# A retention layer's per-head steps, some of them moved to a later slot between the matmuls

## The chip, the cores and the metric

One Trainium2 chip, one core of it. The metric is the device time of one launch in microseconds (us), lower is better. Engines are named as in the profile: PE is TensorE, DVE VectorE, ACT ScalarE, POOL GpSimd, SP SyncE, which here only issues DMAs.

## The reference

Two decoder layers run over 256 prompt tokens and 8 x 4 sample tokens, 288 columns in all. The first layer mixes by attention, the second by retention; each is followed by an MLP with squared ReLU, and every part stands between RMS norms. All of it is float32. The part that matters here is the mixer of the second layer, for each of 4 heads:

```
z = h @ w_in;  q, k rotated (256 wide), v (512 wide), gate (512 wide)
a = (q k^T) * decay;   o = a v + (q * q_dec) S;   S' = c_dec S + (k * k_dec)^T v
mu = mean(o);  var = mean((o - mu)^2);  o = (o - mu) * rsqrt(var + 1e-5)
y = silu(gate) * o;   out = y @ w_out
```

The states S' of the prompt and of the 8 sample sequences are outputs too.

## The kernel before

Activations lie transposed, features on partitions and the 288 tokens in the free dimension. The weights stream through in 121 strips of 1 MB. Each strip is loaded by SP, rounded by ACT (`wH`, line 1092, `round_strip`), and DVE subtracts the rounded part from it (`wL`, line 1412, `split_strip`), so that three fp32r matmuls (lines 558 to 560) give the precision of one in float32. A strip is 48 matmuls: two output tiles (m = 0, 1), eight k-tiles, three products. `wH` and `wL` have two slots. So strip s + 2 is rounded only when the matmuls of strip s are done, and split after that.

The retention layer has 24 input strips (p = 0 to 23) and 8 output strips (p = 24 to 31). The per-head work is cut into steps and laid between the matmuls of the strips: `head_step(p, j)` on PE is called three times in a strip: j = 0 after 18 matmuls, j = 1 after 33, j = 2 after all 48. Heads begin at p = 4, 9, 14 and 20 (`HEAD_AT`); i = 3 (p - start) + j counts a head's steps. Each engine has its own `head_step` with the same numbering, and takes its instructions strictly in the written order:

- PE: steps at their place among the matmuls.
- ACT, for each strip p: step j = 0, step j = 1, then `round_strip` of p + 2, then, where strip p belongs to the gate (p = 8, 9, 14, 15, 20 to 23), Silu over the new gate columns (line 1388), then step j = 2.
- DVE, for each strip p: steps j = 0 and 1, then it takes strip p's result out of its bank (lines 1464 to 1471 or 1823), then step j = 2, then `split_strip` of p + 2.

The steps that bear on the change, for head h. On PE, i = 0 is `turn_v` (eight transposes of the new prompt values into banks 6 and 7, line 881) and `turn_k` (four transposes of the keys into bank 5, line 891, once the root of the head before has been taken out of bank 5). i = 1 is `turn_pad_k` (line 906, waits for ACT's copy of the values), `head_scores` (line 928) and `turn_new_v` (four transposes of the samples' values into bank 5, line 897, once the keys are copied out). i = 2 is `turn_pad_v` (line 916). i = 3 begins with `prompt_state(h, 0)` (line 934), which waits for all four copies of the head (`r_tok` at 4h + 4). ACT has the copies: `copy_tokens` (values, line 1297, and keys, line 1301) at i = 0, `copy_stack_k` (line 1312) and `copy_new_v` (line 1306) at i = 1, `copy_stack_v` (line 1317) at i = 2.

A head ends with its group norm: i = 12 is `mean(h, 0)` on PE (line 993, bank 5), then DVE centres (line 1764), ACT squares (line 1345), and DVE sums (lines 1758 and 1760); i = 14, the end of a head's fifth strip, is `mean(h, 1)` on PE and `head_root` on ACT (line 1349, square root out of bank 5 into `rms`). DVE's `scale` (reciprocal, line 1769, and product, line 1771) comes at j = 0 of the strip after; `times_gate` (line 1777), ACT's `round_y` (line 1353) and `split_y` (line 1781) follow one or more strips later, for the last head in strip 25. For heads 0 and 1 the strip after the fifth is the first of the next head; for head 2 it is strip 19, which has no other step in it, and for head 3 it is strip 25, the second of the output projection.

Silu and the square root need different tables of ACT, so there is an ACT_TABLE_LOAD ahead of each change between them.

Of the kernel before, what the change touches and what calls it, by code (L numbers as in the profile page):

```python
# [101 lines left out]
HEAD_AT = (4, 9, 14, 20)  # L102
# [24 lines left out]
def build_program(nc, wst, x_in, cols, trig, mats, pmask, dmask, rmask, qkdec, kcache, vcache, state,  # L127
                  x_out, k_out, v_out, pstate_out, sstate_out):
    with ExitStack() as ctx:
# [416 lines left out]
        def _(pe):  # L546
# [98 lines left out]
            def turn_new_v(ii):  # L645
                for c in range(2):
                    for i in ii:
                        if i == 6 and c:
                            continue
                        at = 256 * (i % 2) + c * P  # L650
                        mm = nc.tensor.matmul(banks[NS * (i // 2):NS * (i // 2) + NS, 7, at:at + P],
                                              vT[:, 2 * i + c, SEQ:T], ident, start=True, stop=True, skip_group_check=True)
                return mm
# [230 lines left out]
            def turn_k(h):  # L884
                pe.wait_ge(rope_out, 1 + 2 * (16 + 2 * h + 1))
                if h:
                    pe.wait_ge(gn_rms, h)
                for z in range(2):
                    for tb in range(2):
                        c = tb * DK + z * P  # L890
                        mm = nc.tensor.transpose(banks[:, 5, c:c + P], kr[:, 2 * (h % 2) + z, tb * P:tb * P + P], ident)
                mm.then_inc(r_turned, 1)
# [17 lines left out]
            def turn_pad_v(h):  # L910
                pe.wait_ge(r_padL, 4 * h + 4)
                pe.wait_ge(r_stack, 2 * h + 1)
                pe.wait_ge(r_decayed, 3 * h + 3)
                for half in range(2):
                    for c in range(4):
                        mm = nc.tensor.transpose(banks[:, 6 + half, c * P:c * P + P],
                                                 vpad[:, c, 4 * half:4 * half + 4, :].rearrange("p a b -> p (a b)"), ident)
                mm.then_inc(r_pturned, 1)
# [72 lines left out]
            def mean(h, e):  # L991
                pe.wait_ge(o_summed, 2 * h + e + 1)
                nc.tensor.matmul(banks[:, 5, 0:T], mean_v, (oc_sb[:, 2, :], o_sb[:, 0, :])[e], start=True,
                                 stop=True).then_inc(gn_mean, 1)

            def head_step(p, j):

                h = max([n for n in range(NHR) if HEAD_AT[n] <= p], default=0)
                i = 3 * (p - HEAD_AT[h]) + j
                if i == 0:  # L1000
                    turn_v(h)
                    turn_k(h)
                if i == 1:
                    turn_pad_k(h)
                    head_scores(h)
                    turn_new_v(h)
                if i == 2:
                    turn_pad_v(h)
                if i == 3:
                    prompt_state(h, 0)  # L1010
                    read_states(4 * h)
                    outers(4 * h, 0)
                if i == 4:
                    prompt_state(h, 1)
                    outers(4 * h, 1)
                if i == 5:
                    out_prompt(h, 0)
                    read_states(4 * h + 1)
                    outers(4 * h + 1, 0)
                if i == 6:  # L1020
                    out_prompt(h, 1)
                    outers(4 * h + 1, 1)
                if i == 7:
                    out_samples(h)
                    read_states(4 * h + 2)
                    outers(4 * h + 2, 0)
                if i == 8:
                    outers(4 * h + 2, 1)
                if i == 10:
                    read_states(4 * h + 3)  # L1030
                    outers(4 * h + 3, 0)
                if i == 11:
                    outers(4 * h + 3, 1)
                    turn_read(h)
                if i == 12:
                    mean(h, 0)
                if i == 14:
                    mean(h, 1)

            def ret_strip(p, s, out, hi, lo, start=True, stop=True):  # L1040

# [19 lines left out]
            for u in range(N_RETOUT):  # L1061
                j, kh = u % 4, u // 4
# [22 lines left out]
        def _(act):  # L1085
# [207 lines left out]
            def copy_tokens(h):  # L1293
                act.wait_ge(r_turned, 3 * h + 1)
                if h:
                    act.wait_ge(r_out, 3 * h)
                nc.scalar.activation(vtok_r[:, :, :], banks[:, 6:8, :], ACT.Copy).then_inc(r_tok, 1)
                act.wait_ge(r_turned, 3 * h + 2)
                for tb in range(2):
                    c = C_KDEC + tb * NHR + h  # L1300
                    nc.scalar.activation(ktok_r[:, tb, :], banks[:, 5, tb * DK:tb * DK + DK], ACT.Copy,
                                         scale=col[:, c:c + 1]).then_inc(r_tok, 1)

            def copy_new_v(h):
                act.wait_ge(r_turned, 3 * h + 3)
                nc.scalar.activation(vtok_s, banks[0:NS, 5, :], ACT.Copy).then_inc(r_tok, 1)
# [8 lines left out]
            def copy_stack_v(h):  # L1315
                act.wait_ge(r_pturned, 2 * h + 2)
                nc.scalar.activation(vst[:, :, :], banks[:, 6:8, :], ACT.Copy).then_inc(r_stack, 1)
# [25 lines left out]
            def square(h):  # L1343
                act.wait_ge(centred, h + 1)
                nc.scalar.activation(o_sb, oc_sb, ACT.Square).then_inc(gn_sq, 1)

            def head_root(h):
                act.wait_ge(gn_mean, 2 * (h + 1))
                nc.scalar.activation(rms[:, :], banks[:, 5, 0:T], ACT.Sqrt, bias=gn_eps).then_inc(gn_rms, 1)

            def round_y(h):
                act.wait_ge(y_gated, h + 1)
                nc.scalar.activation(yH[:, 4 * h:4 * h + 4, :], oc_sb, ACT.Copy).then_inc(yr_round, 1)

            def head_step(p, j):
                h = max([n for n in range(NHR) if HEAD_AT[n] <= p], default=0)
                i = 3 * (p - HEAD_AT[h]) + j
                if p + 1 in HEAD_AT and j == 2:
                    pad_head(HEAD_AT.index(p + 1))
                if p in GATE_AT and j == 0:  # L1360
                    round_y(GATE_AT.index(p))
                if i == 0:
                    copy_tokens(h)
                if i == 1:
                    copy_stack_k(h)
                    copy_new_v(h)
                if i == 2:
                    copy_stack_v(h)
                if i in (3, 4):
                    copy_state(h, i - 3)  # L1370
                if i in (5, 6, 7):
                    copy_o(h, i - 5)
                if i == 10:
                    copy_read(h)
                if i == 12:
                    square(h)
                if i == 14:
                    head_root(h)

            for p in range(N_RETIN):  # L1380
                c = RET_ORDER[p]
# [27 lines left out]
        def _(dve):  # L1409
# [159 lines left out]
            for i in range(6):  # L1569
                p = P_V + i  # L1570
# [196 lines left out]
            def scale(h):  # L1767
                dve.wait_ge(gn_rms, h + 1)
                nc.vector.reciprocal(rs_post[:, :], rms[:, :]).then_inc(gn_rs, 1)
                dve.wait_ge(gn_rs, 2 * h + 1)  # L1770
                nc.vector.tensor_tensor(oc_sb, oc_sb, rs_post[:, :].unsqueeze(1).broadcast_to([P, 4, T]),
                                        ALU.mult).then_inc(gn_rs, 1)
# [11 lines left out]
            def head_step(p, j):  # L1784
                h = max([n for n in range(NHR) if HEAD_AT[n] <= p], default=0)
                i = 3 * (p - HEAD_AT[h]) + j
                if p + 1 in HEAD_AT and j == 2:
                    own_columns(HEAD_AT.index(p + 1))
                if i == 0:
                    pad_low(h)  # L1790
                if p - 5 in HEAD_AT and j == 0:
                    scale(HEAD_AT.index(p - 5))
                if p in GATE_AT and j == 0:
                    times_gate(GATE_AT.index(p))
                if p in GATE_AT and j == 1:
                    split_y(GATE_AT.index(p))
                if i == 1:
                    decay(h)
                if 3 <= i <= 8:
                    update(4 * h + (i - 3) // 2, (i - 3) % 2)  # L1800
                if i in (10, 11):
                    update(4 * h + 3, i - 10)
                if i == 11:
                    add_read(h)
                    sum_tiles(h, 0)
                if i == 12:
                    centre(h)
                    sum_tiles(h, 1)

            for p in range(N_RETIN):  # L1810
# [4 lines left out]
                if c < 8:  # L1815
                    h = c % NHR
# [202 lines left out]
```

## Time and profile before

| what | value |
|---|---|
| median of 3 runs | 1084.83 us (1083.73 to 1433.3) |
| the profiled execution's own time | 1085.45 us |
| its span | 1083.6 us |
| busy PE, DVE, ACT, POOL | 991.0, 609.4, 433.7, 67.5 us |
| share of PE in the chain that ended last | 83% |
| granted TensorE clock, mean | 0.964 of full speed |
| read and written | 181.39 and 24.33 MB, 190 GB/s over the span |

Busy time is the time in which an engine executed something; matmuls are pipelined, so one row of a matmul overlaps the next. The start-to-start distance of two rows tells what one costs. In rows of the timeline the bracket is the time in which the engine sat idle before the row, and who released it. The retention layer with its heads lies between about 566 and 815 us of the span.

### The profile page before, as it was taken

How to read it: one execution, taken by the hardware profiler on the slowest of the kernel's cores; microseconds unless marked ns; L12 is line 12 of the kernel's file. 1: busy time of each engine (PE TensorE's matmuls, PEld its weight loads, DVE VectorE, ACT ScalarE, POOL GpSimd, SP SyncE). 2: the span in 40 equal slices, each digit the busy share in tenths (PEclk: the TensorE clock that was granted, in tenths of full speed). 3: DMA queues.
4: the chain of work that ended last, by engine and by line, in shares of the span. 5: the costliest groups of instructions: out<-in, count | busy, mean ns of one | idle time of the engine just before them, and what ended most of it. 6: DMA issues, size and time to landing. Idle time of an engine off the chain costs nothing.

```text
span 1083.6 us, 17374 instructions
## 1 busy us (share of the span) xinstructions
PE 991.0 (91%) x7340; PEld 896.4 (83%) x7340; DVE 609.4 (56%) x753; ACT 433.7 (40%) x541; POOL 67.5 (6%) x104
## 2 busy tenths in 40 slices
PE   4999999998769999999689999999999699999993
PEld 4988998654759999999587877778789599999993
DVE  4756653356377555333675667576573765653343
ACT  5222243256444454333334262534343445543330
POOL 3310000000020000000110000000100200000000
PEclk9999999699889999999899999999999899999997
DMA  9787859425524454455534847675665145444411
GB/s 360 262 283 260 274 169 374 149 88 186 204 78 155 159 179 166 157 165 183 188 132 165 305 186 270 242 259 215 243 243 165 69 165 185 156 160 172 173 39 44
DMA packets 50156, 206.60 MB, mean 191 GB/s; under 512 B 3504, under 2 KB 3888, under 8 KB 34224
## 3 DMA queue, kind: packets, MB, share of 16 engines
q1 hardware_dynamic: 44352, 181.40, 48.3%
q0 software_dynamic: 5744, 24.33, 5.7%
q8 instruction: 46, 0.75, 0.3%
q14 instruction: 14, 0.11, 0.0%
HBM read 181.39 MB, written 24.33 MB: 190 GB/s over the span
## 4 chain that ended last, share of the span: by engine, by line
PE 83%; DVE 10%; ACT 4%; issue 1%; POOL 1%; DMA 0%; SPq 0%; DVEq 0%; POOLq 0%; ACTq 0%
PE banks L558 22%; PE banks L559 22%; PE banks L560 22%; PE banks L683 3%; DVE wL L1412 2%; DVE hL L1421 2%; PE banks L970 1%; PE banks L616 1%; DVE tmp L1437 1%; DVE x L1441 1%; PE banks L934 1%; PE banks L727 1%; PE banks L782 1%; PE banks L743 1%; PE banks L981 1%
## 5 line engine op out<-in xcount | busy, mean ns | idle before, releaser
L558 PE MATMUL banks<-hH,wH 128*128 128x288 f32 x1296 | 395.4, 305 | 42.9 <-DVE hL L1421 22.0
L1412 DVE TENSOR_TENSOR wL<-raw,wH 128x2048 fp32r<-128x2048 f32 x120 | 276.8, 2306 | 209.3 <-ACT wH L1092 208.9
L1092 ACT ACTIVATE wH<-raw 128x2048 fp32r<-128x2048 f32 x120 | 229.9, 1916 | 395.4 <-PE banks L560 395.4
L559 PE MATMUL banks<-hL,wH 128*128 128x288 f32 x1296 | 386.2, 298 | 0.0
L560 PE MATMUL banks<-hH,wL 128*128 128x288 f32 x1296 | 386.0, 298 | 0.0
L558 PEld LDWEIGHTS banks<-hH,wH 128*128 128x128 f32 x1296 | 248.8, 192 | 66.6 <-issue 48.4
L559 PEld LDWEIGHTS banks<-hL,wH 128*128 128x128 f32 x1296 | 248.1, 191 | 0.5
L560 PEld LDWEIGHTS banks<-hH,wL 128*128 128x128 f32 x1296 | 247.5, 191 | 0.0
L559 PE MATMUL banks<-aL,wH 128*128 128x288 f32 x512 | 151.0, 295 | 0.0
L560 PE MATMUL banks<-aH,wL 128*128 128x288 f32 x512 | 150.9, 295 | 0.0
L558 PE MATMUL banks<-aH,wH 128*128 128x288 f32 x512 | 150.2, 293 | 0.0
L559 PEld LDWEIGHTS banks<-aL,wH 128*128 128x128 f32 x512 | 96.3, 188 | 0.0
L558 PEld LDWEIGHTS banks<-aH,wH 128*128 128x128 f32 x512 | 96.3, 188 | 0.0
L560 PEld LDWEIGHTS banks<-aH,wL 128*128 128x128 f32 x512 | 96.2, 188 | 0.0
L1484 DVE SCALAR_TENSOR_TENSOR relu_sb<-banks,norms 128x576 f32<-128x576 f32 x32 | 24.2, 758 | 44.3 <-PE banks L560 43.6
L1735 DVE SCALAR_TENSOR_TENSOR sslot<-sslot,banks 128x1024 f32<-128x1024 f32 x22 | 26.8, 1219 | 28.7 <-PE banks L981 28.7
L558 PE MATMUL banks<-yH,wH 128*128 128x288 f32 x128 | 38.1, 298 | 0.0
L559 PE MATMUL banks<-yL,wH 128*128 128x288 f32 x128 | 37.8, 295 | 0.0
L560 PE MATMUL banks<-yH,wL 128*128 128x288 f32 x128 | 37.7, 295 | 0.0
L1464 DVE TENSOR_TENSOR sqacc<-banks,trigs 128x576 f32<-128x576 f32 x24 | 18.1, 755 | 31.6 <-PE banks L560 31.3
L683 PE MATMUL banks<-kT,qT 32*128 32x256 f32 (+1 forms) x256 | 30.3, 370 | 0.0
L492 POOL TENSOR_TENSOR norms<-norms,sqacc 128x288 f32<-128x288 f32 x28 | 28.7, 1025 | 14.3 <-ACT sqacc L1110 13.5
(245 smaller groups left out, 961.1 us busy)
## 6 DMA issues: line engine op xcount, KB each, us to landing
raw<-wst SPq DMA_DIRECT2D x121, 1024.0 KB, 4.8
cache_sb<-kcache SPq DMA_DIRECT2D x14, 1024.0 KB, 6.1
sslot<-state SPq DMA_DIRECT2D x11, 1024.0 KB, 7.1
sstate_out<-sslot POOLq DMA_DIRECT2D x11, 1024.0 KB, 8.5
raw<-vcache SPq DMA_DIRECT2D x6, 1024.0 KB, 9.6
cache_sb<-vcache SPq DMA_DIRECT2D x6, 1024.0 KB, 6.9
raw<-state SPq DMA_DIRECT2D x5, 1024.0 KB, 8.1
sstate_out<-raw POOLq DMA_DIRECT2D x5, 1024.0 KB, 5.5
```

The source lines that it names most:

```text
L492: nc.gpsimd.tensor_tensor(sumsq[:, :], sumsq[:, :], sq[:, k % 2, :], ALU.add).then_inc(xacc, 1)
L558: nc.tensor.matmul(out[:, m, :], wH[:, u % 2, c], hi[:, k, :], start=first, stop=False)
L559: nc.tensor.matmul(out[:, m, :], wH[:, u % 2, c], lo[:, k, :], start=False, stop=False)
L560: return nc.tensor.matmul(out[:, m, :], wL[:, u % 2, c], hi[:, k, :], start=False, stop=last)
L616: mm = nc.tensor.matmul(banks[32 * q:32 * q + 32, 4 + 2 * g + hf, k0 % CPART:k0 % CPART + kn], qz(br, j // 2)[:, j % 2, P * g + 32 * q:P * ...
L683: return nc.tensor.matmul(out, qT[r, t, qq], kT[r, t, kk], start=z == 0, stop=z == 1)
L1092: nc.scalar.activation(wH[:, at % SPL, :], raw[:, raw_slot(at), :], ACT.Copy).then_inc(h_round, 1)
L1412: nc.vector.tensor_tensor(wL[:, at % SPL, :], raw[:, raw_slot(at), :], wH[:, at % SPL, :].bitcast(F32), ALU.subtract).then_inc(l_split, 1)
L1421: nc.vector.scalar_tensor_tensor(out=hL[:, k, :], in0=x[:, k, :], scalar=gain(layer, norm, k), in1=hH[:, k, :].bitcast(F32), op0=ALU.mult, ...
L1464: nc.vector.tensor_tensor(sq[:, :, :], G(u), both(trigR[:, 0, :]), ALU.mult).then_inc(rope_mul, 1)
L1484: nc.vector.scalar_tensor_tensor(out=relu_sb[:, u % 2, :, :], in0=G(u), scalar=0.0, in1=both(rs_pre[:, :]), op0=ALU.max, op1=ALU.mult).the ...
L1735: nc.vector.scalar_tensor_tensor(out=c, in0=c, scalar=GAMMA[u // 4] ** NT, in1=banks[:, 6:8, :], op0=ALU.mult, op1=ALU.add).then_inc(r_upd ...
```

## The change

Five pieces of the per-head work change their slot, and no instruction is added or removed, and no DMA is moved. The mean of squares, `mean(h, 1)`, goes from the end of the head's fifth strip to j = 0 of the strip after, ahead of `turn_v` of the next head where there is one; ACT's `head_root` goes with it, and DVE's `scale` goes from j = 0 to j = 1 there, behind `decay` of the next head. `turn_k` goes from i = 0 to i = 1 and its copies, now `copy_keys`, too, behind `copy_stack_k`. `turn_new_v` and `copy_new_v` go from i = 1 to i = 2.

```diff
 PE, head_step
+                if p - 5 in HEAD_AT and j == 0:
+                    mean(HEAD_AT.index(p - 5), 1)
                 if i == 0:
                     turn_v(h)
-                    turn_k(h)
                 if i == 1:
                     turn_pad_k(h)
                     head_scores(h)
-                    turn_new_v(h)
+                    turn_k(h)
                 if i == 2:
                     turn_pad_v(h)
+                    turn_new_v(h)
...
-                if i == 14:
-                    mean(h, 1)
 ACT, head_step
+                if p - 5 in HEAD_AT and j == 0:
+                    head_root(HEAD_AT.index(p - 5))
                 if i == 0:
                     copy_tokens(h)
                 if i == 1:
                     copy_stack_k(h)
-                    copy_new_v(h)
+                    copy_keys(h)
                 if i == 2:
                     copy_stack_v(h)
+                    copy_new_v(h)
...
-                if i == 14:
-                    head_root(h)
 DVE, head_step
-                if p - 5 in HEAD_AT and j == 0:
-                    scale(HEAD_AT.index(p - 5))
...
                 if i == 1:
                     decay(h)
+                if p - 5 in HEAD_AT and j == 1:
+                    scale(HEAD_AT.index(p - 5))
```

## Rows read from the trace of the kernel before

**Rows 1.** The page, busy time, share of the span and instructions by engine.

```profile
PE 991.0 (91%) x7340; PEld 896.4 (83%) x7340; DVE 609.4 (56%) x753; ACT 433.7 (40%) x541; POOL 67.5 (6%) x104
```

**Rows 2.** Waits of PE, 600 to 830 us: total, times, longest.

```profile
PE banks L993 <- DVE y L1760: 6.7, 5, 1.7
```

**Rows 3.** Timeline, end of strip 8: start, duration, engine, line, instruction.

```profile
622.01 0.29 PE L560 MATMUL banks<-hH,wL 128*128 128x288 f32 x1
...
623.05 0.46 DVE L1760 TENSOR_TENSOR y<-y 128x288 f32<-128x288 f32 x1
...
623.56 0.75 PE L993 MATMUL banks<-y,mat 128*128 128x288 f32 x2 [1.26 <-DVE y L1760]
623.93 0.51 PE L558 MATMUL banks<-hH,wH 128*128 128x288 f32 x1
```

**Rows 4.** Timeline, strip 9, the first of head 1.

```profile
627.02 1.28 ACT L1349 ACT_TABLE_LOAD   x1
...
628.31 0.50 ACT L1349 ACTIVATE norms<-banks,col 128x288 f32<-128x288 f32 x1
628.71 1.02 ACT L1297 ACTIVATE vtok_r<-banks 128x1024 f32<-128x1024 f32 x1
...
628.96 0.63 PE L891 MATMUL banks<-mat,kr 128*128 128x128 f32 x4 [1.39 <-ACT norms L1349]
629.34 0.38 PE L558 MATMUL banks<-hH,wH 128*128 128x288 f32 x1
...
630.83 1.36 DVE L1771 TENSOR_TENSOR y<-y,norms 128x1152 f32<-128x1152 f32 x1
631.41 0.60 PE L906 MATMUL banks<-mat,kpad 128*128 128x128 f32 x4
```

**Rows 5.** Timeline, around the end of strip 9.

```profile
634.14 0.59 ACT L1306 ACTIVATE mat<-banks 32x512 f32<-32x512 f32 x1 [1.50 <-PE banks L897]
635.95 1.03 PE L916 MATMUL banks<-mat,vpad 128*128 128x128 f32 x8
...
639.20 1.02 PE L934 MATMUL banks<-vtok_r,ktok_r 128*128 128x512 f32 x2
...
640.03 1.00 ACT L1317 ACTIVATE vst<-banks 128x1024 fp32r<-128x1024 f32 x1
```

**Rows 6.** Timeline, the same place in head 0, around the end of strip 4.

```profile
578.59 1.04 PE L916 MATMUL banks<-mat,vpad 128*128 128x128 f32 x8
...
580.67 1.00 ACT L1317 ACTIVATE vst<-banks 128x1024 fp32r<-128x1024 f32 x1
...
581.85 1.88 PE L934 MATMUL banks<-vtok_r,ktok_r 128*128 128x512 f32 x4
```

**Rows 7.** Timeline, strip 14, the first of head 2.

```profile
683.86 0.50 ACT L1349 ACTIVATE norms<-banks,col 128x288 f32<-128x288 f32 x1
...
687.17 0.60 PE L906 MATMUL banks<-mat,kpad 128*128 128x128 f32 x4
```

**Rows 8.** Timeline, strips 25 to 27, the norm of head 3.

```profile
803.63 1.95 DVE L1769 RECIPROCAL norms<-norms 128x288 f32<-128x288 f32 x1
...
811.40 2.29 DVE L1412 TENSOR_TENSOR wL<-raw,wH 128x2048 fp32r<-128x2048 f32 x1 [0.45 <-ACT wH L1092]
...
813.90 0.32 PE L558 MATMUL banks<-yH,wH 128*128 128x288 f32 x1
```

**Rows 9.** Timeline, start of the program: ACT's first table load.

```profile
0.75 1.28 ACT L1117 ACT_TABLE_LOAD   x1 [0.75 <-PEq L1999]
...
0.89 0.30 DVE L1495 MEMSET norms<- 128x288 f32 x1 [0.89 <-PEq L1999]
```

**Rows 10.** Windows: busy by engine, then granted clock, DMA share, GB/s.

```profile
628.00:632.00 4.00, 3.04 (x24) 3.07 (x25) 3.12 (x2) 2.45 (x5) 0.00 (x0) 1.00 1.03 398
...
852.00:856.00 4.00, 1.49 (x6) 1.46 (x6) 3.96 (x9) 2.38 (x6) 1.73 (x2) 0.50 0.00 0
856.00:860.00 4.00, 3.73 (x15) 2.87 (x13) 4.00 (x8) 1.97 (x5) 2.07 (x3) 0.57 0.00 0
```

More of the change, by code:

```diff
@@ L1297, in copy_tokens, with copy_keys @@
                 nc.scalar.activation(vtok_r[:, :, :], banks[:, 6:8, :], ACT.Copy).then_inc(r_tok, 1)
+            def copy_keys(h):
                 act.wait_ge(r_turned, 3 * h + 2)
```

## The prediction

> **What bounds the kernel now.** The page's first part comes first: PE is busy 91% of the span [rows 1], and the retention layer is a string of strips with little room between them. So a wait of PE there is paid in full, and a wait of any other engine is free until PE has to wait for it. The second view is PE's waits in the stretch of the heads. They are nearly all one kind: the mean (line 993) waiting for DVE's last sum, five times, 6.7 us [rows 2]. The longest, 1.7 us, is the first mean of head 2, which the change doesn't touch; the other four are the second mean of each head, at the end of strips 8, 13, 18 and 24, with the remaining 5.0 us in nearly equal parts (1.26 in strip 8 [rows 3]). The third view is the timeline around each. At the end of strip 8 the last matmul starts at 622.01, and the first of strip 9 at 623.93 [rows 3]. Matmuls follow each other every 0.13 us (15 between 629.34 and 631.41, the first 0.1 longer [rows 4]). So strip 9 could have begun at 622.14, and the mean costs PE 1.79 us there, of which 0.37 (623.56 to 623.93) is its own work and 1.42 the wait with its restart.
>
> **The change, part by part.** Times are those of the trace; strips keep their numbers.
>
> *The second mean later.* It will be issued 18 matmuls into the next strip, 18 x 0.13 = 2.4 us after 622.14, at 624.5. DVE's sum ends at 623.51 [rows 3]. No wait is left: -1.42 us for strips 8, 13 and 18, and at first for 24. Its own 0.37 us stays (0.09 more in strip 19, where it interrupts the matmuls alone).
>
> *What holds head 1 instead.* After mean and `turn_v` (1.3 us) and 15 matmuls (2.07), PE reaches `turn_pad_k` at about 627.9. This waits for ACT's copy of the values, which stands behind the root on ACT. ACT is no earlier than before: Silu of strip 8 and the padding hold it to 627.02, then table load, root and copy run to 629.73 [rows 4]. From the end of an ACT instruction to PE's start is 0.15 us (root ends 628.81, PE starts 628.96 [rows 4]). So `turn_pad_k` starts at 629.88 instead of 631.41, **1.53 us earlier**. The old wait of `turn_k` (1.39 us [rows 4]) is gone, but a new one of nearly 2 us stands one slot later.
>
> *Head 2.* Without the wait (1.42), without `turn_k` in slot 0 (0.38, from 628.96 to 629.34 [rows 4]) and without one restart (0.1), `turn_pad_k` would start 1.9 us before 687.17, at 685.27. The root still starts at 683.86 [rows 7]; 0.40 later the copy of the values, 1.02 long, and 0.15: ready at 685.43. **1.74 us earlier.**
>
> *Head 3.* The mean is in strip 19, which has no other step, the root has a whole strip of time, and nothing holds `turn_pad_k`: 1.42 + 0.38 - 0.09, **1.7 us earlier**. Head 0 has no mean ahead of it: 0.36 us earlier, only because `turn_k` left slot 0.
>
> *Keys in slot 1, new values in slot 2.* From `turn_pad_k` to the end of the strip nothing changes, four transposes stand for four. After the end come `turn_pad_v` and now `turn_new_v`: 0.37 us more before the next strip. Its copy is where the cost is. Today ACT copies the new values at 634.14, inside the strip [rows 5]. In slot 2 it stands on ACT behind the rounding of strip p + 2, which starts only when strip p is done, behind Silu with its table load, and behind `copy_stack_v`. That one starts at 640.03, 4.08 us after `turn_pad_v` at 635.95 [rows 5]. The next ACT instruction starts 0.09 before its end (as 628.71 behind the root [rows 4]), the copy takes 0.59 [rows 5], PE follows 0.15 later: 4.08 + 0.91 + 0.59 + 0.15 = 5.73 us. `prompt_state(h, 0)` needs it, and stands now at 3.25 us (635.95 to 639.20 [rows 5]), or 3.25 + 0.37 = 3.62 with `turn_new_v` in front. **PE waits 2.11 us**, in heads 1, 2 and 3, whose first strips are gate strips all three. Against today `prompt_state` comes 5.73 - 3.25 = 2.48 us later after the strip's end.
>
> *Head 0.* Strip 4 is a key strip, without Silu: `copy_stack_v` starts 2.08 us after `turn_pad_v`, and `prompt_state` 3.26 after it [rows 6]. 2.08 + 0.91 + 0.59 + 0.15 = 3.73: 0.47 later than today, of which 0.11 is a wait.
>
> *DVE's scale behind decay.* Reciprocal (1.95 [rows 8]) and product (1.36 [rows 4]) now stand after `decay`, which ends some 1.7 us before the strip's end (15 matmuls and four transposes after the scores, less three small products). They end 1.6 us after the strip's end, so the strip's result is taken out about 1.5 us late, by 2.4 us after. Costed at nothing: its users are Silu, whose table load ends 3.4 us after the strip's end, and the strip after the next, more than 6 us off. With that cover gone the price is up to 1.5 us a head.
>
> *Head 3's norm.* Here I expect the gain to be taken back. Strips 25 and 26 run 1.4 us earlier, but strip 27 needs its split. Today DVE's reciprocal (803.63) stands right behind the split of strip 26, then scale, gate, ACT's rounding of y, then the rounding of strip 27, then its split, which starts at 811.40 and ends at 813.69; strip 27 begins at 813.90, with no time over [rows 8]. No link of that chain moves forward: it starts with the rounding of strip 26 at the end of strip 24. So strip 27 begins when it did, and the last 1.42 us are lost: **0**. That the chain gets no longer depends on the root's table load being done before the mean arrives. The trace has it so: ACT's first load starts at 0.75, ahead of the memset (0.89) for which ACT waits by the code before that activation [rows 9]. If it had to wait behind the mean, the root would be some 0.65 us later there.
>
> *Sum.* Shift of `prompt_state` against today, per head: head 0 -0.36 + 0.47 = +0.11; head 1 -1.53 + 2.48 = +0.95; head 2 -1.74 + 2.48 = +0.74; head 3 -1.70 + 2.48 = +0.78; end 0. Together **+2.6 us**. Bounds: a fully hidden copy of the new values gives, with 0.37 us for `turn_new_v` back, -1.16 - 1.37 - 1.33 = -3.9 us; table loads behind their waits add 0.65 at the end and 0.3 each in heads 1 and 2, +3.9. I take +2.6, because each duration in it is read at its own place and the order on ACT is fixed by the code. Against the profiled execution that is 1085.45 + 2.6 = 1088.0; the median is 0.6 lower, so 1087.4, and I say 1087.5.
>
> **Table loads.** The trace's load takes 1.28 us, and the root follows at once (627.02 + 1.28 = 628.30, root at 628.31 [rows 4]). The Trainium skill, page ScalarE: Activation LUTs, section What ACT_TABLE_LOAD costs, gives about 1.28 us for the load and about 1.38 more for a drain, 2.66 in all; no such drain stands between the two rows, and by the page each of the three gate heads would pay an estimated 1.4 us more. The order of Silu and root doesn't change, so there are eight loads as before.
>
> **The rivals.**
>
> *The copy is hidden, not slower but faster.* The four waits of the mean are gone and nothing comes in their place at `prompt_state`: -3.9 us, 1081. It decides at a wait of about 1.2 us: below that, a head gains. For it speaks that the mean's waits are the only ones the waits view shows; against it that ACT reaches `copy_stack_v` at 640.03, after PE's `prompt_state` at 639.20 [rows 5], and the new copy comes after that. Chance 0.10.
>
> *The end keeps its gain.* Strip 27 gets its split earlier, because another order of DVE and ACT lets it: +2.6 - 1.4 = +1.2, 1086.0. Against: the chain of rows 8 has only 0.45 us of idle in its last link. Chance 0.10.
>
> *A table change costs a second load's time where it isn't hidden.* In the three gate heads the chain to `copy_new_v` grows by 1.28: +2.6 + 3.8, 1091.3. This would be the direction of the page just named. Rows 4 speak against it. Chance 0.04.
>
> *The clock falls in the new waits.* PE worked 1.49 + 3.73 us at about half clock, 1.2 GHz, after a long idle stretch at the last layer's start, which costs about 2.6 us a time [rows 10]. Three falls: +2.6 + 7.8, 1095.2. The 1.39 us wait before 628.96 left the clock at 1.00, the 2.4 GHz level [rows 10], and the new ones are little longer. Chance 0.03.
>
> **How the numbers follow.** Forecast 0.70, the rivals 0.10, 0.10, 0.04 and 0.03, and 0.03 for what I don't see. The range takes in the forecast with its table bound and run-to-run scatter, and the rival at 1086.0: 1083.8 to 1090.5, about 0.8. It leaves out the faster rival below and the two dear ones above. 2%, about what a measurement of this kernel can tell from no change, is 21.7 us; no case reaches it: within 2% 0.98, 0.01 on each side.
>
> **What would show it.** In the changed kernel's waits PE should have no line 993 wait but the one of head 2's first mean; a wait of about 2.1 us of line 934 for ACT line 1306, three times, and a tiny one in head 0; a wait of nearly 2 us of line 906 for ACT line 1297 in head 1, and about 0.2 in head 2; and about 1.4 us of line 558 for DVE line 1412 near 814 us. `scale` should end after the first strip of heads 1 and 2, with no PE wait from it. Line 934 without a wait would prove the main step wrong; so would a wait of line 881 or a lower clock in 566 to 815.

## The result: 0.3% slower, and the profile after

The changed kernel takes 1088.04 us (median of 13 runs, 1085.56 to 1092.25), the kernel before 1085.13 us on the same chip. The ratio of the two is 1.0029, with a 95% interval from 1.0017 to 1.0040. The forecast was 1087.5 us, 2.6 us slower; the medians differ by 2.9 us, and the ratio says about 3.1 (1.8 to 4.3 by its interval). Three of the 13 runs of the kernel before were slow (1433 to 5425 us), and the ratio leaves them out.

PE's waits between 600 and 830 us, in the changed kernel: total, times, longest.

```profile
PE banks L934 <- ACT mat L1308: 5.3, 3, 1.8
PE banks L906 <- ACT vtok_r L1297: 1.9, 1, 1.9
PE banks L993 <- DVE y L1763: 1.7, 1, 1.7
PE banks L558 <- DVE wL L1415: 1.3, 1, 1.3
```

This is the answer to [rows 2]. The 6.7 us of line 993 has shrunk to the one wait of 1.7 us that the change doesn't touch. In its place stand three other kinds: `prompt_state` (line 934) for the copy of the new values, three times; `turn_pad_k` (line 906) for the copy of the values; a strip for its split. Line numbers of ACT and DVE behind the edits are one to three higher than before (1306 is now 1308, 1412 is 1415).

The timeline of the changed kernel at the start of head 1, the answer to [rows 3] and [rows 4]:

```profile
625.63 0.65 PE L993 MATMUL banks<-y,mat 128*128 128x288 f32 x2
626.12 1.04 PE L881 MATMUL banks<-mat,vTr 128*128 128x128 f32 x8
...
628.15 1.28 ACT L1351 ACT_TABLE_LOAD   x1
...
629.44 0.50 ACT L1351 ACTIVATE norms<-banks,col 128x288 f32<-128x288 f32 x1
629.84 1.02 ACT L1297 ACTIVATE vtok_r<-banks 128x1024 f32<-128x1024 f32 x1
631.00 0.63 PE L906 MATMUL banks<-mat,kpad 128*128 128x128 f32 x4 [1.86 <-ACT vtok_r L1297]
```

The mean finds its sum ready and has no bracket. But line 906 waits 1.86 us for a copy that stands on ACT behind table load and root.

The end of strip 9 in the changed kernel, the answer to [rows 5]:

```profile
635.61 1.04 PE L916 MATMUL banks<-mat,vpad 128*128 128x128 f32 x8
...
635.87 1.92 ACT L1092 ACTIVATE wH<-raw 128x2048 fp32r<-128x2048 f32 x1 [1.22 <-PE banks L560]
636.48 0.60 PE L897 MATMUL banks<-mat,vTr 128*32 128x128 f32 x4
...
637.80 1.28 ACT L1391 ACT_TABLE_LOAD   x1
...
639.10 0.68 ACT L1391 ACTIVATE gate<-gate 128x576 f32<-128x576 f32 x1
639.69 1.01 ACT L1319 ACTIVATE vst<-banks 128x1024 fp32r<-128x1024 f32 x1
...
640.59 0.57 ACT L1308 ACTIVATE mat<-banks 32x512 f32<-32x512 f32 x1
641.21 1.98 PE L934 MATMUL banks<-vtok_r,ktok_r 128*128 128x512 f32 x4 [1.74 <-ACT mat L1308]
```

The new values are transposed at 636.48, and ACT takes them only at 640.59, after rounding, table load, Silu and stack copy; then PE starts 0.05 us after the copy's end. From `turn_pad_v` to `prompt_state` it is 5.60 us here, against 3.25 in [rows 5].

And strip 27, the answer to [rows 8]:

```profile
814.81 2.29 DVE L1415 TENSOR_TENSOR wL<-raw,wH 128x2048 fp32r<-128x2048 f32 x1 [0.45 <-ACT wH L1092]
...
817.25 0.37 PE L558 MATMUL banks<-yH,wH 128*128 128x288 f32 x1 [1.28 <-DVE wL L1415]
```

**Reading small differences.** Whole runs scatter by several microseconds, which is as much as any part here. A stretch inside the trace doesn't. I read each kernel from the moment DVE takes strip 3's result, just ahead of head 0, to two marks: the first matmul of strip 27, and the mean of line 564 after the mixer. These rows are the start mark and the second mark, first of the kernel before, then of the changed kernel.

```profile
568.58 0.76 DVE L1823 TENSOR_TENSOR vTr<-banks,norms 128x576 f32<-128x576 f32 x1 [2.01 <-PE banks L560]
...
848.38 0.75 PE L564 MATMUL banks<-sqacc,mat 128*128 128x288 f32 x2 [2.57 <-DVE sqacc L1457]
```

```profile
569.65 0.76 DVE L1826 TENSOR_TENSOR vTr<-banks,norms 128x576 f32<-128x576 f32 x1 [2.01 <-PE banks L560]
...
851.79 1.33 PE L564 MATMUL banks<-sqacc,mat 128*128 128x288 f32 x2 [2.57 <-DVE sqacc L1460]
```

The distances from the start mark, for the two kernels and for the experiments below (a field is left empty where no row was read for it):

| kernel | to strip 27, us | to line 564, us | against before |
|---|---|---|---|
| before | 245.32 | 279.80 | |
| changed | 247.60 | 282.14 | +2.34 |
| `scale_back` | 247.66 | 282.19 | +2.39 |
| `end_late` | | 280.67 | +0.87 |
| `end_before` | | 279.83 | +0.03 |
| `slots_only` | | 284.96 | +5.16 |
| `norm_only` | 243.59 | 278.13 | -1.67 |
| `copy_first` | 241.58 | 276.13 | -3.67 |
| `tokens_first` | 239.53 | 274.07 | -5.73 |
| `best` | | 272.53 | -7.27 |

How well such a distance repeats is seen in kernels whose instructions are the same up to a point. The `prompt_state` of head 3 stands 190.19 us behind the start mark in the kernel before and 190.23 in `end_before`, 192.44 in the changed kernel and 192.49 in `end_late`: 0.05 us over some 190. Only `copy_first` and `best` were also timed in six runs each; of the other experiments there is one execution, so only the stretch in its trace is compared. The spans of the two profiled executions differ by 3.8 us: 2.3 of it is this stretch, 1.1 lies ahead of it and 0.4 behind it, where no instruction was moved.

### The profile page after: what moved, and what is told of

Its sections match the earlier page's. It is cut to its first block, busy times and chain, and to the rows that moved or that the text cites. A ratio compares the mean times of both kernels' runs of the same rounds, so it can differ in the third digit from the quotient of the medians.

```text
span 1087.4 us, 17374 instructions
## 1 busy us (share of the span) xinstructions
PE 993.4 (91%) x7340; PEld 897.7 (83%) x7340; DVE 608.8 (56%) x753; ACT 433.7 (40%) x541; POOL 67.4 (6%) x104
## 4 chain that ended last, share of the span: by engine, by line
PE 81%; DVE 10%; ACT 5%; issue 2%; POOL 1%; DMA 0%; SPq 0%; DVEq 0%; ACTq 0%; POOLq 0%
PE banks L558 22%; PE banks L559 21%; PE banks L560 21%; PE banks L683 3%; DVE wL L1415 2%; ACT wH L1092 2%; DVE hL L1424 2%; PE banks L970 1%; PE banks L616 1%; DVE tmp L1440 1%; DVE x L1444 1%; PE banks L934 1%; PE banks L727 1%; PE banks L782 1%; DVE norms L1420 1%
```

## The experiments

**The copy ahead of Silu: `copy_first`.** The main step was that the new values' copy stands at the wrong place in ACT's queue. So only that was changed.

```diff
 ACT, in strip p
                 round_strip(S_RETIN + p + SPL, S_RETIN + p + SPL)
+                if p in HEAD_AT:
+                    copy_new_v(HEAD_AT.index(p))
                 if c >= 16:
 ACT, head_step
                 if i == 2:
                     copy_stack_v(h)
-                    copy_new_v(h)
```

> The changed kernel with one edit: ACT copies the new values right behind the rounding of strip p + 2, ahead of Silu and the stack copy. Read as the stage from DVE taking strip 3's result to the first matmul of strip 27 (245.3 us before the change, 247.6 after). Theory (prompt_state waits for this copy because of its place in ACT's queue): no wait of line 934 for ACT is left, about 2.0 us less in each of heads 1 to 3, stage 241.7, 3.6 us under the kernel before, ratio about 0.997. Rival (PE at that place is bound by the stack copy and Silu anyway, which come 0.5 us later here): the outer products of line 981 wait in place of line 934, less than half is won, stage 245 or more.

Measured: 1083.16 us against 1086.26, ratio 0.9971 (0.9953 to 0.9989); to strip 27 241.58, where the theory said 241.7. The timeline of this kernel at the same place:

```profile
636.17 1.04 PE L916 MATMUL banks<-mat,vpad 128*128 128x128 f32 x8
636.43 1.92 ACT L1092 ACTIVATE wH<-raw 128x2048 fp32r<-128x2048 f32 x1 [1.23 <-PE banks L560]
637.04 0.60 PE L897 MATMUL banks<-mat,vTr 128*32 128x128 f32 x4
...
638.25 0.57 ACT L1308 ACTIVATE mat<-banks 32x512 f32<-32x512 f32 x1
...
639.87 1.88 PE L934 MATMUL banks<-vtok_r,ktok_r 128*128 128x512 f32 x4
...
640.72 1.01 ACT L1319 ACTIVATE vst<-banks 128x1024 fp32r<-128x1024 f32 x1
...
642.67 0.50 PE L981 MATMUL banks<-vst,kst 32*128 32x512 f32 x2
```

Line 934 comes 3.70 us after line 916, without a bracket. The stack copy is about 0.5 us later than it was and still in time for line 981. The rival falls. The three waits were worth 6.0 us, 2.0 each: line 934 stands 1.9 us nearer to line 916 (3.70 against 5.60), and its four matmuls take 1.88 us where they took 1.98 behind the wait. The 6.0 us are more than the 2.3 us by which the change lost: the order on one queue decided its sign.

**The keys and new values alone: `slots_only`.** Mean, root and scale are back where they were.

```diff
 PE, head_step
-                if p - 5 in HEAD_AT and j == 0:
-                    mean(HEAD_AT.index(p - 5), 1)
...
+                if i == 14:
+                    mean(h, 1)
 (ACT's head_root and DVE's scale likewise)
```

> Keys and new values in their later slots, as changed, but mean, root and scale at their old places. Theory (the parts interact through ACT's queue): head 1 as in the changed kernel, +0.9 us, because the copy of the values is bound by root and table load either way; heads 2 and 3 about +2.0 each; nothing at the end; stage 245.3 + 4.9 = 250.2. Rival (each mean's wait is worth its full 1.4 us whatever else moves): the changed kernel's 247.6 + 4 x 1.4 = 253.2.

Measured: 284.96 to line 564, 5.16 us more than before. Strip 27 has no wait here, so the 34.48 us that lie between the marks in the kernel before put it at 250.5 (expected 250.2).

```profile
PE banks L993 <- DVE y L1763: 6.7, 5, 1.7
PE banks L934 <- ACT mat L1308: 5.3, 3, 1.8
PE banks L906 <- ACT vtok_r L1297: 0.3, 1, 0.3
```

Both kinds of wait stand side by side. In head 1 line 906 starts 61.37 us after the start mark, in the changed kernel 61.35: with the mean's wait and without it, the time is the same, because ACT's chain binds there.

**The norm alone: `norm_only`.** The other half of the change.

```diff
 PE, head_step
                 if i == 0:
                     turn_v(h)
+                    turn_k(h)
                 if i == 1:
                     turn_pad_k(h)
                     head_scores(h)
-                    turn_k(h)
+                    turn_new_v(h)
                 if i == 2:
                     turn_pad_v(h)
-                    turn_new_v(h)
 (ACT's copies likewise)
```

> Mean, root and scale one step later, as changed, but keys and new values in their old slots. Theory (what follows a mean's wait takes up its gain): turn_k waits for the root instead, about 3 us in head 1 and 1.2 in head 2; head 1 wins 0, head 2 about 0.2, head 3 1.3, the end 0, because strip 27 waits for its split; stage 243.8. Rival (the gains stay): 4 x 1.4 less, stage 239.7.

Measured: to strip 27 243.59 (expected 243.8), -1.7 us. PE's waits from 560 to 850 us:

```profile
PE banks L891 <- ACT norms L1351: 4.1, 2, 2.9
PE banks L564 <- DVE sqacc L1460: 2.6, 1, 2.6
PE banks L993 <- DVE y L1763: 1.7, 1, 1.7
PE banks L558 <- DVE wL L1415: 1.3, 1, 1.3
```

Four waits of 1.25 us are gone. The wait for the root has grown from 1.4 us to 4.1, and 1.3 us for the split of strip 27 has come. Of some 5.7 us less than two are left: nothing in head 1, 0.2 us in head 2 and 1.5 in head 3, as expected.

The halves don't add up: -1.67 and +5.16 make +3.49, together they are +2.34. Nearly all of the difference lies in head 2. There the norm alone moves `prompt_state` by -0.2 us and the slots alone by +2.1, but both together by +0.79: with the keys in their later slot line 891 no longer waits for the root (1.1 us in `norm_only`), and the mean's gain is kept. In head 1 the two halves give 0 and about +0.95, and together +0.90: there the wait for the root is replaced by that for the values' copy, and nothing is won.

**DVE's scale back ahead of decay: `scale_back`.**

```diff
 DVE, head_step
+                if p - 5 in HEAD_AT and j == 0:
+                    scale(HEAD_AT.index(p - 5))
...
-                if p - 5 in HEAD_AT and j == 1:
-                    scale(HEAD_AT.index(p - 5))
```

> The changed kernel with DVE's scale back at the slot before decay. Theory (DVE has cover on both sides): stage 247.6 within 0.3, no new wait of PE. Rival (scale behind decay makes DVE's taking of the strip's result late and this costs): up to 1.5 us less in heads 1 and 2, stage 244.6 to 246.

Measured: 247.66, the same waits. What was costed at nothing costs nothing.

**The last head's norm behind strip 27: `end_late` and `end_before`.** The same edit was made on the changed kernel and on the kernel before.

```diff
 ACT, output strips
-                if u == 1:
-                    round_y(NHR - 1)
                 down(2, S_RETOUT + u, RET_GROUP.get(u), u == N_RETOUT - 1)
+                if u == 1:
+                    round_y(NHR - 1)
 DVE, output strips
                 if u == 1:
                     times_gate(NHR - 1)
-                    split_y(NHR - 1)
                 down(2, S_RETOUT + u, RET_GROUP.get(u), u == N_RETOUT - 1, 8)
+                if u == 1:
+                    split_y(NHR - 1)
```

> The changed kernel with the rounding of y and its split behind the rounding and split of strip 27. Theory (strip 27 waits because its rounding and split stand behind the last head's norm): the 1.28 us wait of line 558 goes, to line 564 282.14 - 1.28 = 280.9. Rival (the wait moves to strip 28, which needs the same queues): 282.1.

> The kernel before with the same edit at strips 25 to 27 alone. Theory (there the split of strip 27 came just in time, so freeing it wins nothing): 279.8 within 0.2. Rival (strip 27 was bound in the kernel before, too): 1 us or more less.

Measured: 280.67 on the changed kernel, 1.47 us less (expected 280.9), with no wait of line 558 in the stretch; 279.83 on the kernel before, 0.03 more. So strip 27 was just in time before, and the change made it a wait of its own: the last mean's gain went there whole.

**The prompt values ahead of the root: `tokens_first`.** On top of `copy_first`:

```diff
 ACT, head_step
-                if p - 5 in HEAD_AT and j == 0:
-                    head_root(HEAD_AT.index(p - 5))
                 if i == 0:
                     copy_tokens(h)
+                if p - 5 in HEAD_AT and j == 0:
+                    head_root(HEAD_AT.index(p - 5))
```

> copy_first with ACT's copy of the prompt values ahead of the root. Theory (turn_pad_k waits in ACT's queue behind root and table load; turn_k, the only user of the root on PE, comes 2.1 us later): to line 564 276.1 - 1.85 = 274.3; the wait of strip 27 stays at 1.28. Rival (turn_k takes over the wait): 276.1 with line 891 waiting 1.5 us or more.

Measured: 274.07, 2.06 us less than `copy_first` (1.85 expected); the wait of line 906 is gone and no wait of line 891 has come for it. Of the 2.06 us 1.8 are won in head 1 and 0.2 in head 2.

**All three edits: `best`.**

> The changed kernel with three edits of order: new values copied ahead of Silu (as in copy_first), ACT's copy of the prompt values ahead of the root, and in strip 25 the rounding of y behind the rounding of strip 27 and its split behind that of strip 27. Read from DVE taking strip 3's result to the mean of line 564 after the mixer (279.8 us before, 282.1 changed, 276.1 copy_first). Theory (each edit frees the one wait that PE has there): copy_first's 276.1, less 1.7 in head 1 and 0.15 in head 2 (0.2 of the 1.9 us wait of line 906 stays), less 1.28 for strip 27: 273.0, 6.8 us under the kernel before, ratio 0.9937. Rival (a root that comes later only moves the wait to turn_k, and the late split of y to strip 28): nothing won over copy_first, 276, ratio 0.997.

Measured: 1077.44 us against 1086.21, ratio 0.9927 (0.9909 to 0.9945); to line 564 272.53 us. It beats both kernels. Its timeline in strip 9:

```profile
626.39 1.01 ACT L1297 ACTIVATE vtok_r<-banks 128x1024 f32<-128x1024 f32 x1
...
627.41 1.28 ACT L1351 ACT_TABLE_LOAD   x1
627.54 0.63 PE L906 MATMUL banks<-mat,kpad 128*128 128x128 f32 x4
...
628.71 0.50 ACT L1351 ACTIVATE norms<-banks,col 128x288 f32<-128x288 f32 x1
...
629.65 0.66 PE L891 MATMUL banks<-mat,kr 128*128 128x128 f32 x4
```

The copy comes first, line 906 doesn't wait, and the root is done 0.44 us before line 891 needs it. Of PE's waits from 560 to 850 us only the last of these rows belongs to a head, the first mean of head 2; the other two stand behind the mixer:

```profile
PE banks L558 <- DVE hL L1425: 5.4, 1, 5.4
PE banks L564 <- DVE sqacc L1461: 2.6, 1, 2.6
PE banks L993 <- DVE y L1764: 1.7, 1, 1.7
```

## Why the prediction was right

It was right in sign and size, and not because large errors cancelled: the waits stand where it put them, and of its five terms the furthest off is 0.26 us away. These are the shifts of `prompt_state` against the kernel before, each without the shift of the head ahead of it (in brackets the distances from the start mark, before and changed):

| step | forecast, us | measured, us |
|---|---|---|
| head 0 | +0.11 | +0.04 (13.27 to 13.31) |
| head 1 | +0.95 | +0.90 (70.62 to 71.56) |
| head 2 | +0.74 | +0.79 (126.38 to 128.11) |
| head 3 | +0.78 | +0.52 (190.19 to 192.44) |
| end, strip 27 | 0 | +0.03 (245.32 to 247.60) |
| sum | +2.6 | +2.28 |

- *The second mean later.* No wait of a second mean is left, in any head.
- *What holds head 1.* `turn_pad_k` was forecast 1.53 us earlier than in the kernel before; from `prompt_state` of head 0 on it came 1.52 earlier, with a wait of 1.86 where nearly 2 was written. Head 2: 1.64 for 1.74, and the 0.1 between them is the time by which the matmuls of line 934 take longer behind their wait (1.98 against 1.88 us). The wait of about 0.2 us forecast for head 2 isn't in the waits view, but the distance of the rows has it: 0.35 us from the last matmul to line 906 where 0.13 is usual, and `tokens_first` wins 0.2 there.

```profile
687.19 0.30 PE L560 MATMUL banks<-hH,wL 128*128 128x288 f32 x1
...
687.54 0.63 PE L906 MATMUL banks<-mat,kpad 128*128 128x128 f32 x4
```

- *Head 3.* 1.87 us earlier instead of 1.70. This is the largest miss. The mean in strip 19 delays the matmuls behind it by 0.27 us (742.11 to 742.51 below, less the usual 0.13), and 0.46 was charged. That `turn_k` left slot 0 gives 0.44 in head 0 (line 906 from 5.47 to 5.03 us behind the start mark) where 0.36 was written. The longer matmuls of line 934 behind the wait, 0.1, go the other way.
- *Head 0.* The wait of 0.11 us isn't there: `prompt_state` stands 13.31 us behind the start mark, and 13.29 in `copy_first`, where its copy comes earlier.
- *The new values' copy.* Forecast 5.73 us after `turn_pad_v`, measured 5.60 in all three heads. The stack copy starts 4.08 us after `turn_pad_v`, as forecast; most of the miss is that PE follows the copy's end by 0.05 us and not by 0.15, the rest that the copy is 0.57 long and not 0.59. Without the wait the distance is 3.70 (`copy_first`) where 3.62 was written, so line 934 is held for 1.90 us and not 2.11; the profile's bracket has 1.74 to 1.76. The three terms together were 0.4 us too dear. Removing the cause gave back 6.0 us.
- *DVE's scale.* Costed at nothing, and `scale_back` shows it.
- *Head 3's norm.* Strip 27 waits 1.28 us (about 1.4 was written), and `end_late` with `end_before` shows the cause.
- *Table loads.* They add nothing, as forecast. In strip 19 of the changed kernel the load starts ahead of the mean for which the root waits:

```profile
742.07 1.28 ACT L1351 ACT_TABLE_LOAD   x1
...
742.11 0.30 PE L560 MATMUL banks<-hH,wL 128*128 128x288 f32 x1
742.25 0.65 PE L993 MATMUL banks<-y,mat 128*128 128x288 f32 x2
...
742.51 0.51 PE L558 MATMUL banks<-hH,wH 128*128 128x288 f32 x1
...
743.36 0.50 ACT L1351 ACTIVATE norms<-banks,col 128x288 f32<-128x288 f32 x1
```

The root follows 1.29 us after the start of the load, with no room for more. The Trainium skill, page ScalarE: Activation LUTs, section What ACT_TABLE_LOAD costs, names a drain of about 1.38 us on top; this trace doesn't show it.

Of the rivals, the hidden copy fell: its 3.9 us under the kernel before are near what `copy_first` reached with the copy moved (3.67). That the end keeps its gain fell with the 1.28 us of line 558. The table rival is told above. The clock rival fell, too. The windows of the changed kernel have their granted clock behind the five busy times:

```profile
600.00:650.00 50.00, 46.27 (x315) 37.87 (x315) 31.39 (x36) 22.24 (x27) 3.37 (x5) 1.00 0.71 258
650.00:700.00 50.00, 48.08 (x335) 40.29 (x337) 33.98 (x42) 21.13 (x25) 3.03 (x4) 1.00 0.76 273
...
750.00:800.00 50.00, 48.05 (x322) 38.17 (x321) 27.96 (x30) 19.39 (x22) 4.13 (x6) 1.00 0.54 198
800.00:820.00 20.00, 18.72 (x141) 18.41 (x140) 15.21 (x11) 9.75 (x7) 0.00 (x0) 1.00 0.52 196
```

The new waits lie in these windows, and the clock stays at 1.00, the level of 2.4 GHz.

## What to carry to other kernels

A step that is moved takes its place in every queue it touches: find out what each engine has written ahead of it there, above all work that can't begin before a point that the old slot lay ahead of. A wait that is removed is worth only what the next wait on the same chain leaves of it; walk that chain to the next moment at which the bounding engine must meet it. And where whole runs scatter by more than the effect, measure between two marks inside the trace.

## What the runs showed of the hardware that I had not expected

The stretch with all four heads in it repeats to within 0.05 us over 190 from one execution to another, as far as the instructions are the same, while the moment at which it starts lay anywhere from 566.20 to 571.54 us in ten kernels whose instructions up to there are the same. Behind the second mark 235.0 to 235.8 us are left in each. So nearly all the scatter of the profiled executions comes from ahead of the heads.

The granted clock goes with it. Its mean from 180 to 220 us was 0.70 in the execution that started latest (`slots_only`, 571.54), 0.74 in the three that started at 569.65 to 570.51, 0.79 in the four at 568.03 to 568.84, and 0.83 in the two earliest (566.20 and 566.84). The windows of `slots_only` and of `end_before`, the latest and the earliest:

```profile
180.00:220.00 40.00, 35.92 (x231) 24.22 (x229) 13.59 (x38) 12.95 (x31) 0.00 (x0) 0.70 0.59 200
```

```profile
180.00:220.00 40.00, 35.49 (x254) 24.11 (x250) 16.57 (x47) 15.13 (x36) 0.00 (x0) 0.83 0.57 195
```

As an estimate, 0.13 of 40 us is 5.2 us of work at the full clock, about the 5.3 us by which the two starts differ. Why the clock stayed low for longer in one execution than in another wasn't tried and stays open.
